# Layer 1 of a two-layer hybrid backbone: the state-space output joined with the product behind it, its norm taken in two halves, and the second norm with its weights set beside

## The reference, cut to what matters

```python
def finish(y, xs, z):                                   # end of the Mamba-2 mixer
    y = y + d_skip[:, None] * xs
    y = y.reshape(Bsz, L, 2048) * silu(z)
    y = rms_norm(y.reshape(Bsz, L, 4, 512), norm_g)     # four groups of 512 features
    return y.reshape(Bsz, L, 2048) @ w_out              # 2048 -> 1024
x = x + gt1 * m_lat
h = modulate(rms_norm(x, norm_ffn_g), sh2, sc2)         # "the second norm"
u = dwconv(h @ w_up, w_conv)                            # 1024 -> 5632, 3 taps over tokens
val, gate = split(u, 2)
x = x + gt2 * ((silu(gate) * val) @ w_down)             # 2816 -> 1024
return rms_norm(x, final_g)
```

## Time and profile before

| | us |
|---|---|
| median of 3 runs | 1547.99 (1546.88 to 1558.4) |
| profiled execution, its own time | 1549.64 |
| its span | 1547.9 |
| PE busy | 1433.3 (93%) |
| DVE busy | 888.5 (57%) |
| ACT busy | 599.7 (39%) |
| POOL busy | 141.9 (9%) |
| TensorE clock granted, mean | 0.964 of full |

### The profile page before, as it was taken

The page is one execution under the profiler, slowest core; times in us unless marked ns, Lnnn a source line. Parts: engine busy times, 40 slices in busy tenths (PEclk is TensorE's granted clock), DMA queues, the critical chain, the costliest instruction groups (busy, mean ns, idle before and its releaser), DMA issues. The chain is left out here.

```text
span 1547.9 us, 30877 instructions
## 1 busy us (share of the span) xinstructions
PE 1433.3 (93%) x13563; PEld 1196.9 (77%) x13563; DVE 888.5 (57%) x1270; ACT 599.7 (39%) x968; POOL 141.9 (9%) x152
## 2 busy tenths in 40 slices
PE   3798999899998999999999999989999999799998
PEld 2566676777887788777778888868887768799998
DVE  3559634545453666555565225787765655688844
ACT  2323444222231244333333124444543554455534
POOL 1000000233242030000000003000002330000000
PEclk8999989899999999999999999999999998899999
DMA  9321101143324233665552322222332003366643
GB/s 328 85 82 55 55 28 41 57 143 135 111 86 137 61 105 84 185 183 174 164 159 86 108 83 89 69 85 79 109 111 80 2 28 129 108 182 182 191 163 109
DMA packets 170257, 172.30 MB, mean 111 GB/s; under 512 B 15271, under 2 KB 135947, under 8 KB 170123
## 3 DMA queue, kind: packets, MB, share of 16 engines
q1 hardware_dynamic: 167728, 165.14, 34.9%
q0 software_dynamic: 1088, 4.19, 0.7%
q10 hardware_dynamic: 1306, 0.99, 0.2%
HBM read 169.26 MB, written 1.05 MB: 110 GB/s over the span
## 5 line engine op out<-in xcount | busy, mean ns | idle before, releaser
L640 PE MATMUL bank<-h,w_hi 128*128 128x256 f32 (+2 forms) x968 | 333.9, 345 | 5.5 <-issue 2.9
L315 DVE TENSOR_TENSOR w_lo<-w_raw,w_hi 128x2048 fp32r<-128x2048 f32 (+1 forms) x94 | 213.8, 2274 | 211.4 <-ACT w_hi L305 211.3
L643 PE MATMUL bank<-h,w_hi 128*128 128x256 f32 (+2 forms) x968 | 325.2, 336 | 0.0
L644 PE MATMUL bank<-h,w_lo 128*128 128x256 f32 (+2 forms) x968 | 325.1, 336 | 0.0
L305 ACT ACTIVATE w_hi<-w_raw 128x2048 fp32r<-128x2048 f32 x95 | 180.2, 1898 | 200.2 <-PE bank L640 147.9
L658 DVE SCALAR_TENSOR_TENSOR acc<-bank,params,acc 128x510 f32<-128x510 f32 (+3 forms) x272 | 173.1, 646 | 86.1 <-ACT acc L1686 60.0
L640 PEld LDWEIGHTS bank<-h,w_hi 128*128 128x128 f32 (+1 forms) x968 | 186.2, 192 | 40.0 <-issue 21.7
L643 PEld LDWEIGHTS bank<-h,w_hi 128*128 128x128 f32 (+1 forms) x968 | 186.1, 192 | 20.1 <-issue 2.9
L644 PEld LDWEIGHTS bank<-h,w_lo 128*128 128x128 f32 (+1 forms) x968 | 185.9, 192 | 18.8
L1686 ACT ACTIVATE acc<-bank,params 128x512 f32<-128x512 f32 (+1 forms) x88 | 48.9, 580 | 152.0 <-PE bank L644 52.4
L640 PE MATMUL bank<-h_hi,w_hi_hyb 128*128 128x512 f32 (+1 forms) x184 | 79.1, 430 | 12.2 <-DVE h_lo L614 4.4
(11 more groups left out here) (417 smaller groups left out, 2858.1 us busy)
## 6 DMA issues: line engine op xcount, KB each, us to landing
w_raw<-in_ffn_up SPq DMA_DIRECT2D x88, 512.0 KB, 5.3
w_raw<-in_mod_w SPq DMA_DIRECT2D x40, 1024.0 KB, 5.3
w_raw<-in_ffn_down SPq DMA_DIRECT2D x22, 1024.0 KB, 4.9
w_raw<-in_ssm_w_in SPq DMA_DIRECT2D x20, 1024.0 KB, 5.3
w_raw<-in_hyb_w_in SPq DMA_DIRECT2D x9, 1024.0 KB, 5.3
w_raw<-in_ssm_w_out SPq DMA_DIRECT2D x8, 1024.0 KB, 4.8
mod_early<-in_mod_w SPq DMA_DIRECT2D x4, 1024.0 KB, 17.6
mod_early<-in_mod_w POOLq DMA_DIRECT2D x4, 1024.0 KB, 14.2
```

Of the source, the lines that this page charges most:

```text
L315: dve.tensor_tensor(lo, raw, hi.bitcast(F32), ALU.subtract).then_inc(k.lo_done.sem, 1)
L640: mm = pe.matmul(out, wh, xh, start=(start and n == 0), stop=False)
L643: pe.matmul(out, wh, xl, start=False, stop=False)
L644: mm = pe.matmul(out, wl, xh, start=False, stop=(stop and n == last))
```

## The change

Of the output norm and product:

- `stage_ssd_out` becomes a class `SsdOut` whose steps run inside the block of `stage_layer1_tail`. No meeting of the engines lies between them any more, and SP's loads of the tail may start while the state-space output still runs.
- `YNorm` is taken in two halves. The sums of groups 0 and 1 (columns 0 to 127 of the sum bank) and of groups 2 and 3 (columns 128 to 255) each have their root, reciprocal, spread and copy on 128 columns. The first half runs before `leave(7)`, `square(7)` and `sums(7)`; the second half's root stands behind high(1) on ACT, its reciprocal behind low(1) on DVE, its spread inside R0 on PE.
- In R0 PE takes banks 0, 1, 2, 4, 5, 6 first, chunk 0 then chunk 1, each as soon as it is there, then the second spread, then banks 3 and 7 (3 is the sum bank, 7 the spread's).
- The splits of R2 to R6 stand behind the chunks of their own slot, where they stood ahead of them.

Of the second norm:

- U0 is an "extra" entry that stands ahead of R7 in the stream, and is split ahead of R7 into `w_hi_extra1` and `w_lo_extra1`. U1 is an ordinary slot; its `split_hi` stands ahead of the squares on ACT, its `split_lo` is cut in two halves on DVE, one ahead of and one behind the norm's reciprocal.
- The five additions of squares move from DVE to GpSimd.

```diff
+def split_lo_half(k, dve, g, h):
+    n = k.stream.plan[g][1]
+    w = slice(h * KD * P, h * KD * P + KD * P)
...
+    ins = dve.tensor_tensor(k.wlo[:, n % 2, w], k.stream.raw[:, g % 2, w], k.whi[:, n % 2, w].bitcast(F32), ALU.subtract)
...
-            if self.ynorm is not None:
+            if self.ynorm is not None and s > 0:
                 pe.wait_ge(self.ynorm.lo_done.sem, self.ynorm.lo_done.at(2 * s + 2))
...
+            if s == 0 and self.ynorm is not None:
+                early, late = (0, 1, 2, 4, 5, 6), (3, 7)
+                for q, m in [(q, m) for ms in (early, late) for q in range(2) for m in ms]:
+                    if m == early[0]:
+                        pe.wait_ge(self.ynorm.lo_done.sem, self.ynorm.lo_done.at(q + 1))
+                    if (q, m) == (0, late[0]):
+                        self.ynorm.pe_spread(pe, 1)
+                    if (q, m) == (0, late[1]):
+                        pe.wait_ge(self.ynorm.copied.sem, self.ynorm.copied.at(2))
+                    split_matmuls(pe, self.bank(m)[:, 0:n], [pair(m, q)], start=(q == 0), stop=False)
...
+    def pool_add(self, pool, j):
+        pool.wait_ge(self.sq_done.sem, self.sq_done.at(j + 1))
+        if j >= 2:
+            pool.wait_ge(self.acc_done.sem, self.acc_done.at(j - 1))
+        first = self.sq[:, 0, :] if j == 1 else self.acc[:, :]
+        pool.tensor_tensor(self.acc[:, :], first, self.sq[:, j % 2, :], ALU.add).then_inc(self.acc_done.sem, 1)
...
     def act(self, act):
+        split_hi(self.k, act, self.slots[1])
         self.act_ready(act)
...
+    def pool(self, pool):
+        for j in range(1, 6):
+            self.squares.pool_add(pool, j)
+
     def dve(self, dve):
-        self.squares.dve_evict_and_add(dve)
+        for m in range(KD):
+            self.row.dve_evict(dve, m)
+        split_lo_half(self.k, dve, self.slots[1], 0)
         self.dve_recip(dve)
+        split_lo_half(self.k, dve, self.slots[1], 1)
         self.dve_modulate(dve)
...
-            for n in ((2, 3), (), ())[s] if self.paired and s < 3 else (s + 1,):
+            for n in ((2, 3), (), ())[s] if self.paired and s < 3 else (s + 1,) if s > 0 else ():
                 split_hi(k, act, self.slots[n])
...
+        def sums(q):
+            pe.wait_ge(self.sq_done.sem, self.sq_done.at(q + 1))
+            if q == 6:
+                pe.wait_ge(self.ynorm.root_done.sem, self.ynorm.root_done.at(1))
...
+        self.ynorm.pe_spread(pe, 0)
+        sums(7)
...
+        act.activation(k.scratch[0:1, 0:1], k.eps[0:1, 0:1], ACT.Sqrt)
+        act.wait_ge(self.sum_done.sem, self.sum_done.at(6))
+        self.ynorm.act_root(act, 0)
+        self.ynorm.act_copy(act, 0)
+        square(7)
...
+        self.ynorm.dve_recip(dve, 0)
+        leave(7)
...
         @block.scalar
         def _(act):
-            ynorm.act_root(act)
+            ssd.act(act)
             for c in range(16):
                 ynorm.act_hi(act, c)
-                if c % 2 == 1:
-                    row1.act_splits(act, c // 2 + 1, c // 2 + 2)
+                if c == 1:
+                    act.wait_ge(ssd.sum_done.sem, ssd.sum_done.at(8))
+                    ynorm.act_root(act, 1)
+                    row1.act_splits(act, 1, 2)
+                    ynorm.act_copy(act, 1)
+                if c >= 5 and c % 2 == 1 and c < 15:
+                    row1.act_splits(act, c // 2, c // 2 + 1)
+            extra_hi(k, act, g_up[0])
+            row1.act_splits(act, 7, 8)
             norm.act(act)
...
-            ynorm.dve_recip(dve)
+            ssd.dve(dve)
             for c in range(17):
                 if c < 16:
                     ynorm.dve_scale(dve, c)
                 if c >= 1:
                     ynorm.dve_lo(dve, c - 1)
-                if c >= 2 and c % 2 == 0:
-                    row1.dve_splits(dve, c // 2, c // 2 + 1)
+                if c == 2:
+                    ynorm.dve_recip(dve, 1)
+                    row1.dve_splits(dve, 1, 2)
+                if c >= 6 and c % 2 == 0 and c < 16:
+                    row1.dve_splits(dve, c // 2 - 1, c // 2)
+            extra_lo(k, dve, g_up[0])
+            row1.dve_splits(dve, 7, 8)
             norm.dve(dve)
...
+        g_sout, ahead = row_loads(k, a["ssm_w_out"][0], SI // P // 2, [up_parts(up1, 0)])
+        g_up1 = pair_loads(k, a["ffn_up"][1], first=ahead)
```

More of the change, by code:

```diff
@@ L1297, with __init__ @@
 class Norm:
-    def __init__(self, k, layer, which, row, hT, lT, b):
-        self.k, self.layer, self.which, self.row = k, layer, which, row
+    def __init__(self, k, layer, which, row, hT, lT, b, slots):
+        self.k, self.layer, self.which, self.row, self.slots = k, layer, which, row, slots
         self.t0, self.n = row.t0, row.n
@@ new lines, in act, with decays, square @@
+    def act(self, act):
+        k, b, units, NU = self.k, self.b, self.units, len(self.units)
+        D, E, Y, S, v4, over = self.D, self.E, self.Y, self.S, self.v4, self.over
+        def decays(u):
+            q, t, dr = units[u]
+            act.wait_ge(self.gr_done.sem, self.gr_done.at(u + 1))
+            if u >= 3:
+                act.wait_ge(self.ap_done.sem, self.ap_done.at(u - 2))
+            for h in range(4):
+                col = dr * SH + 4 * q + h
+                ins = act.activation(b.dec[:, u % 3, h, :], D(u)[:, h * P:h * P + P], ACT.Exp, bias=b.gcols[:, 4, 2 + t, col:col + 1])
+            ins.then_inc(self.de_done.sem, 1)
+        def square(q):
+            act.wait_ge(self.y_done.sem, self.y_done.at(q + 1))
+            if q >= 2:
+                act.wait_ge(self.sum_done.sem, self.sum_done.at(q - 1))
+            act.activation(b.sqy[:, q % 2, :], b.y[:, 2 * q:2 * q + 2, :].rearrange("p c n -> p (c n)"), ACT.Square).then_inc(self.sq_done.sem, 1)
+        for u in range(NU):
+            decays(u)
+            if u >= 6 and u % 4 == 2:
+                square(u // 4 - 1)
+            if u == 20:
+                split_hi(k, act, self.first)
+        act.activation(k.scratch[0:1, 0:1], k.eps[0:1, 0:1], ACT.Sqrt)
[3 more added lines that the diff above has]
+        square(7)
@@ L3060, in act_root @@
-    def act_root(self, act):
-        act.activation(self.b.rr[:, :], self.k.pb[7][:, 0:LL], ACT.Sqrt, bias=self.k.eps[:, 0:1], scale=1.0 / 512).then_inc(self.root_done.sem, 1)
-        for i in range(2):
-            act.wait_ge(self.spread_done.sem, self.spread_done.at(i + 1))
-            act.activation(self.b.rs[:, i, :], self.k.pb[i][:, :], ACT.Copy).then_inc(self.copied.sem, 1)
+        pe.wait_ge(self.recip_done.sem, self.recip_done.at(p + 1))
+        for i in range(4):
+            mm = pe.matmul(self.spread_bank()[:, i * P:i * P + P], bc(k.ident[:, 32 * i:32 * i + 1], [P, P]),
+                           self.b.rr[:, p * P:p * P + P], start=True, stop=True)
@@ L3066, in act_hi, with act_root, act_copy @@
+        mm.then_inc(self.spread_done.sem, 1)
+    def act_root(self, act, p):
+        w = slice(p * P, p * P + P)
+        act.activation(self.b.rr[:, w], self.k.pb[7][:, w], ACT.Sqrt, bias=self.k.eps[:, 0:1], scale=1.0 / 512).then_inc(self.root_done.sem, 1)
+    def act_copy(self, act, p):
+        act.wait_ge(self.spread_done.sem, self.spread_done.at(p + 1))
+        act.activation(self.b.rs[:, p, :], self.spread_bank()[:, :], ACT.Copy).then_inc(self.copied.sem, 1)
     def act_hi(self, act, c):
@@ L3184, in _ @@
         def _(pe):
[L3185 removed]
+            ssd.pe(pe)
             row1.pe(pe)
@@ L3217, in _ @@
             fin.dve(dve)
+        @block.gpsimd
+        def _(pool):
+            ssd.pool(pool)
+            norm.pool(pool)
 TALLIES = {
```

329 lines of the change are left out of this document (153 added, 176 removed).

## The result

| | before | changed |
|---|---|---|
| median, us | 1549.89 (4 runs, 1546.88 to 1558.4) | 1535.46 (4 runs, 1533.45 to 1536.45) |
| ratio | | 0.9886, 95% interval 0.9843 to 0.993 |
| span of the profiled execution | 1547.9 | 1531.7 |

Faster by 1.1%. The ratio with its interval is estimated from the single runs; it isn't the quotient of the two medians, which is 0.9907. The median lies 3.6 us under my forecast, inside its range. By the ratio the change passes the bound of 1%, to which I had given 7 in 100; by the medians it doesn't, and the interval lies on both sides of it. The spans differ by 16.2 us, where I had 8.9. From the last y of the state-space stage (`leave(7)`) to U1 it came out nearly as drawn, so I looked ahead of it.

What follows compares the result with a forecast made beforehand. Time is lost where engines take turns around the output product and second norm; PE paces the feed-forward. Cumulative gains of 6.1 at R0, 9.5 at R6, 7.5 at R7, 7.9 at U0 and 8.9 at U2 gave 1539.1 us; range 1533.5 to 1543.5.

Steps and rivals of the forecast that it cites:

- the kernel's end moves by the same 8.9: Behind U2 PE is busy throughout, so the 8.9 us gained there passes unchanged to the kernel's end.
- everything falls well: Larger-gain rival: no collision, short low stretch in U0, no down-product fall, quick R7 load; 14.1 us, 1533.9; chance 0.15.
- no pause under 2 us brings a fall: Clock reading: a fall follows a 2.0 us pause in the down product, none shorter; so none in R0.
- The rival of the merged block that brings nothing: At the output product's start, sums(7) wait for the full norm; R0 near 1278, 4 us lost, 1543; chance 0.05.
- that of the clock in R0: Clock falls in R0 for 3.4 us, costing 1.5; chance 0.17 shared with chunks holding the slots, 1541 to 1543.
- R1 to R6 at 5.76, paced by PE: Output product: splits behind chunks need 5.2 us, so slots take 5.76 instead of 6.31; gain 9.5 at R6.
- my 6.8: Gain at R1's start in the output product: 1281.7 us instead of 1288.46.
- R7's stall: R7's load may start only when R6 is split: 2.5 us wait, R7 at 1318.8, gain there 7.5.
- no stretch of 0.50 before 1325: Sign: from R0's start near 1274, PE's clock shows no low stretch before 1325 us.
- U1's landing, GpSimd's chain last, and one collision: Second norm: U1's load lands at 1319.9, GpSimd's additions end latest, and one half-split collision costs 1.0 us.
- my 1328.9: Time of the second norm's last PE sums, collision included, instead of 1336.80: 7.9 us gained.
- my 3.4 to 6.8: Range for the low-clock stretch in U0, taken as 5.2 us; either end shifts the result by 0.8.

Runs made afterwards that it cites:

- run 2: Kernel before with only the sums of squares of y and their spread regrouped, four products of 128 columns in two column groups: 1548.23 us, ratio 0.997.
- run 3: Changed kernel without its second norm's part: 1542.26 us, ratio 0.9938 to the kernel before.
- run 8: Kernel of run 3 with the splits of R2 to R7 back ahead of the chunks of their own slot: 1543.97 us, ratio 0.9963.
- run 7: Kernel of run 6 with U0's load and splits moved behind those of R7: 1537.13 us, ratio 0.9911.
- run 11: Changed kernel with both halves of U1's low part behind the norm's reciprocal: 1542.92 us, ratio 0.9928.
- run 1: Changed kernel again, unchanged, in eight runs: 1539.5 us against 1553.52 before, ratio 0.9923.
- run 12: Changed kernel a third time, unchanged: 1541.11 us against 1554.02 before, ratio 0.9924.
- run 5: Changed kernel with the five additions of squares back on VectorE: 1540.98 us against 1550.51 before, ratio 0.9936.
- run 6: Kernel of run 5 with U1's w_hi behind the root on ACT, its low halves into and behind the norm's chunks: 1537.57 us, ratio 0.9901.
- run 4: Kernel before with the second norm's part alone: 1551.43 us, ratio 0.9989.
- run 10: Kernel of run 7 with U0's low part in halves, ahead of the evictions and behind the reciprocal: 1537.19 us against 1554.02 before, ratio 0.9884.

## Why the prediction was right or wrong

**The step that failed is a term left out.** "The change part by part" begins at R0. The sums of the state-space stage stand in the diff (4 products into two column groups instead of 2 into one), and I read them only as the halves of the norm. They stand among work that PE itself paces, so nearly all of the 0.42 us by which each sum is shorter comes off the cycle of a q: six lie between the first and the last y, 2.3 us as measured, and 0.6 behind it (run 2: 81.3 to 80.7). I priced it at nothing, without naming a cover. A second term is missing with the other sign: "the kernel's end moves by the same 8.9", but from the final norm's last sums to the end it takes 7.2 us in the four profiles with the separate block and 7.7 to 7.8 in the ten with the merged one, 0.5 more. The second store of the output is issued 0.70 us behind the first there, where it was 0.42; why is open. With both my sum would be 11.3 us: at 1553.5 it gives 0.9927, where the two larger samples show 0.9923 and 0.9924.

**The rest of the difference is the sample.** The spans differ by 1.8 ahead of the first x_skip (same code), 2.8 by the clock up to the first y, 2.3 by the sums, 8.3 from the last y to U1 (81.3 less 73.0) and 1.0 behind it. The 1.0 is 1.5 by the clock, less the 0.5 at the end: behind the same pause of 2 us in the down product before ran 16 matmuls at 0.21 us, the changed kernel's first profile none. Eleven of the fourteen profiles of this study have that low stretch; the changed kernel's first and those of runs 3 and 8 haven't. The prediction had it as one item of "everything falls well". In all fourteen profiles of this study the window of that clock is either all at 0.50 and the interval 15.7 or 15.8 us (eight, before and seven others), or all at 1.00 and 12.9 or 13.0 (six: the three of the changed kernel, runs 2, 7 and 11); run 2 has the old steps there, run 3 the new ones. The first x_skip lies anywhere from 1186.8 to 1197.0, before at 1188.6. I had compared my sum to one execution, and had read in its trace that no pause under 2 us brings a fall; to a change of clock ahead of the first y, in work that the diff doesn't touch, I gave no chance. So the passing of 1% in the first four runs is a matter of the sample, as far as the intervals can tell; by the larger ones the change is worth 0.8%.

**Behind the last y** I compare distances from it (forecast: 1269.7), since all ahead of it is told above:

| | forecast | first profile |
|---|---|---|
| R0 | 4.3 | 3.8 |
| R1 | 12.0 | 11.5 |
| R6 | 40.8 | 40.4 |
| R7 | 49.1 | 48.6 |
| PE sums of bank 7 in the norm | 59.2 | 59.7 |
| U0 | 64.2 | 64.5 |
| U1 | 72.3 | 73.0 |

- R0: the half norm ahead of `leave(7)` and the last sums behind the copy, as drawn; the clock did not fall (1.00 throughout from 1262 to 1310). The two sums that PE makes behind the last y's product are 0.42 shorter each; of this 0.5 reached R0, which then waited 0.37 for the low part of chunk 0 on DVE [0.37 <-DVE y_lo L3149], a wait that the forecast did not have. The rival of the merged block that brings nothing is out, and so is that of the clock in R0.
- R1 to R6 at 5.76, paced by PE: right, and run 8 gives the cause. R1 of before starts at 1288.30 in PE's timeline, not at the 1288.46 of the chain's row, so R1 gained 0.2 less than my 6.8 and the slots behind it 0.2 more.
- R7's stall: 8.2 against 8.3, by the load. Right, and run 7 gives its price. The sign "no stretch of 0.50 before 1325" failed: R7 ran 15 matmuls at 0.21 us in the first profile. Behind the same stall runs 1 and 12 show none. It made the evictions later by 1.5, as the prediction allowed, and they still ended ahead of GpSimd.
- U1's landing, GpSimd's chain last, and one collision: each as written, the collision 1.0 in the first profile and 0.5 and 0.8 in the others; runs 5 and 11 show the last two. The chain's row at 1321.92 is the first of twelve products; the four of bank 7, for which my 1328.9 stood, start at 1322.43, so what makes U0 late lies ahead of them. What I did not see is how the three hang together: run 6 on top of run 5 brought only 0.2, and run 4 even gained.
- U0 ran at 0.21 us a matmul for 6.1 us instead of 5.2, within my 3.4 to 6.8, and took 8.5 in all instead of 8.1; in runs 1 and 12 the low stretch was 5.3 and 3.8 us, U0 8.2 and 7.5. No pause ahead of U1: right.
- Behind U1 the profiles take 196.0 to 197.5 us to the end, before 197.0, the changed kernel's first the least, its two others 197.4: the low stretch in the down product and the 0.5 at the end, as told above.

**What stays open.** From x_skip to U1 the rows account for 10.7 us (2.3, and 8.4 as the mean of three profiles), or 11.4 with the best of the three, and 0.5 of it is lost at the end; the ratios say 12, with 4 to 6 to either side. Why the clock falls in some executions and not in others, ahead of the first y, in R7 and in the down product, was not tried. That it has nothing to do with the code ahead of the first y is shown by one profile each way: run 2 has the old steps and the high clock, run 3 the new ones and the low. The gain of run 10 over the changed kernel is shown in the traces; in the times the intervals still touch.

## What to carry to other kernels

Go through the diff line by line and put a price on each, also where a line seems only to rename or regroup; a product that PE does among its own paced work costs nearly its full length in each round. Before a difference between two profiles is explained, compare the stretches of same code: here those ahead of the first y and in the down product held 6.1 of 16.2 us. A step that makes PE pause can also cost a low stretch behind the pause, in some executions and not in others, and a single profile of an experiment shows only one of the two. And of a change with several parts, follow each in the trace to what ends last: by the traces the second norm's part, as built, spent on R7's stall and on GpSimd's chain more than it gained.

## What the runs showed of the hardware

Two products with 32 columns of weights each, in different column groups, ran nearly side by side: four of them into two groups took 0.63 us, into one 1.06. Three pauses of PE were followed by a low clock in some profiles and not in others: one of 1.7 us ahead of the first y (0.50 for six microseconds in eight of fourteen profiles, 1.00 in six, worth 2.8 us), one of 2.3 us ahead of R7 in the changed kernel (15 matmuls at 0.21 us in its first profile, none in the two others), and one of 2 us in the down product (a low stretch in eleven of fourteen, worth 1.5 us). In U0 the low stretch lasted 6.1, 5.3 and 3.8 us in the three profiles of the changed kernel. The Trainium skill (TensorE: Matmul & The Clock Gate, Part 1) says that the number of slow matmuls at a start differs from run to run of the same kernel, and these three agree.

An addition on GpSimd with two SBUF inputs took 0.72 to 0.74 us, and 1.27 to 1.77 where a VectorE split with two SBUF inputs ran beside it; evictions with one operand in PSUM held none up.
